# A three-block kernel on one core: query tokens, rotary product, gate product and column sums are computed another way, and three tables of work order are new

## What is computed

```
proj = h @ w_in                                  # h: 528 x 1024
p_rwkv, p_diff, p_gate = split(proj)
# RWKV branch: the gate
g = sigmoid(gd) @ g2                             # gd: 528 x 160, g2: 160 x 1024
y = (y + bonus) * g
# differential attention, 8 heads, each with two score maps
q, k = partial_rope(q), partial_rope(k)          # the first 16 of 64 rows of each half head turn
x1, x2 = x[..., :8], x[..., 8:16]
rot = [x1 * cos - x2 * sin, x2 * cos + x1 * sin]
o = concatenate([meta_out, outs])                # queries 0..15, then 4 blocks of 128 queries
merged = gates0 * (o_rwkv @ W) + gates1 * (o_diff @ W')
h_res = h_res + merged @ w_out
h = rms_norm(h_res)                              # needs the sum over 1024 rows of h_res**2
h_res = h_res + square(relu(h @ w1)) @ w2
out = rms_norm(h_res)[:, 16:]                    # the 16 meta tokens are dropped
```

## Time and profile before

| | |
|---|---|
| median of 3 runs | 3085.76 us (3073.72 to 3088.74) |
| profiled execution, its own time | 3070.59 us |
| its span | 3068.7 us |
| mean granted TensorE clock | 0.952 |

### The profile page before, as it was taken

How to read it: one execution, slowest core, us unless ns; L and a number is a source line. 1 busy time by engine, 2 the same in 40 slices (tenths; PEclk the granted TensorE clock), 3 DMA queues, 4 the chain that set the end, 5 groups by cost and what they waited for, 6 DMA issues and landing times.

```text
span 3068.7 us, 53994 instructions
## 1 busy us (share of the span) xinstructions
PE 2826.4 (92%) x22582; PEld 2275.8 (74%) x22582; DVE 1601.6 (52%) x2907; ACT 1215.1 (40%) x2134; POOL 849.2 (28%) x849
## 2 busy tenths in 40 slices
PE   7899999989998999999989988998897999899997
PEld 7788888878876877887667777776775888566565
DVE  4545644555432544343244446456666899844553
ACT  2423433342331233233242434353325777534341
POOL 5222222212224200000143535353100027454233
PEclk9989998999899999999998999999999999899999
DMA  4111111111114332333121212221433888421122
GB/s 140 36 33 42 34 40 36 39 29 40 39 51 172 117 110 89 96 95 91 51 66 52 80 51 77 63 76 55 158 100 123 327 318 335 167 76 56 42 59 69
DMA packets 104003, 286.24 MB, mean 93 GB/s; under 512 B 11696, under 2 KB 11824, under 8 KB 102480
## 3 DMA queue, kind: packets, MB, share of 16 engines
q1 hardware_dynamic: 83408, 209.11, 22.2%
q0 software_dynamic: 15024, 62.14, 5.5%
q10 hardware_dynamic: 5328, 11.54, 1.0%
HBM read 262.81 MB, written 19.92 MB: 92 GB/s over the span
## 4 chain that ended last, share of the span: by engine, by line
PE 70%; DVE 17%; ACT 9%; issue 2%; DMA 2%; ACTq 0%; DVEq 0%; SPq 0%; POOLq 0%
PE psum L497 68%; DVE arena L429 9%; ACT arena L414 4%; ACT arena L422 3%; DVE arena L438 3%; PE psum L501 2%; ACT L409 1%; DVE ring L429 1%; DMA ring<-in_w 1%; DVE arena L433 1%; DVE arena L441 1%; DVE arena L453 0%; DVE arena L450 0%; DMA arena<-in_x 0%; DVE arena L457 0%
## 5 line engine op out<-in xcount | busy, mean ns | idle before, releaser
L497 PE MATMUL psum<-arena,ring 128*128 128x512 f32 (+3 forms) x6280 | 1453.9, 365 | 16.9 <-DVE arena L429 6.0
L497 PEld LDWEIGHTS psum<-arena,ring 128*128 128x128 f32 (+2 forms) x6280 | 1047.3, 193 | 210.9 <-issue 36.8
L497 PE MATMUL psum<-arena 32*32 32x32 f32 (+18 forms) x12332 | 798.8, 244 | 138.2 <-DVE arena L429 46.1
L497 PE MATMUL psum<-arena,arena 128*128 128x512 f32 (+2 forms) x3004 | 844.3, 386 | 37.0 <-DVE arena L429 15.1
L497 PEld LDWEIGHTS psum<-arena 32*32 32x32 f32 (+10 forms) x12332 | 581.4, 136 | 322.1 <-issue 113.4
L497 PEld LDWEIGHTS psum<-arena,arena 128*128 128x128 f32 x3004 | 541.4, 189 | 171.4 <-issue 25.2
L441 POOL CAST ring<-ring 128x512 fp32r<-128x512 f32 x348 | 234.6, 674 | 1357.1 <-DMA ring<-in_w 1213.5
L422 ACT ACTIVATE arena<-psum 128x512 f32<-128x512 f32 (+12 forms) x682 | 295.3, 450 | 752.0 <-PE psum L497 598.4
L429 DVE TENSOR_TENSOR arena<-arena 128x256 f32<-128x256 f32 (+8 forms) x681 | 361.8, 544 | 229.7 <-ACT arena L414 115.9
L429 POOL TENSOR_TENSOR ring<-ring,ring 128x512 fp32r<-128x512 f32 x348 | 465.8, 1338 | 28.0
L414 ACT ACTIVATE arena<-arena 128x512 f32<-128x512 f32 (+10 forms) x532 | 305.2, 583 | 343.0 <-DVE arena L429 160.9
(11 more groups left out here) (52 smaller groups left out, 843.6 us busy)
## 6 DMA issues: line engine op xcount, KB each, us to landing
ring<-in_w SPq DMA_DIRECT2D x372, 256.0 KB, 2.7
ring<-in_w SPq DMA_DIRECT2D x133, 512.0 KB, 3.5
arena<-in_w SPq DMA_DIRECT2D x61, 512.0 KB, 5.5
bg<-arena ACTq DMA_DIRECT2D x24, 256.0 KB, 2.2
yd<-arena ACTq DMA_DIRECT2D x7, 512.0 KB, 7.2
arena<-bg POOLq DMA_DIRECT2D x1, 3072.0 KB, 16.8
arena<-in_x SPq DMA_DIRECT2D x1, 2112.0 KB, 8.1
od<-arena POOLq DMA_DIRECT2D x8, 256.0 KB, 2.3
```

The source lines that it names most:

```text
L497: self.last_ins = self.eng.matmul(out, l, r, start=start, stop=stop, skip_group_check=skip)
```

## The change

Seven parts:

1. Queries of the 16 meta tokens are no longer computed in the attention: q is projected for 512 tokens in one bank (24 matmuls of 512 columns in place of 48 of 264), the 16-query tile goes, and the head's last column sum is over 512 tokens.
2. Rotary: the product with `rot` goes; four small DMAs, issued by ACT after its copy, move 8 rows each to their partner's place in `d.rot` (the signs are in `sin` now). `d.rot` shares the tile `d.P[3]`.
3. The gate's last 32 rows: weights and activations are laid out three times on 96 rows (high, high, low on high, low, high) and multiplied once in fp32r. The third low-rank tile is computed with 96 rows in place of 32, and DVE makes the parts once (7 instructions) before the heads begin.
4. The MLP's first column sum: POOL adds tiles 0 to 6, PE sums two operands in place of 8.
5. The sums at the MLP's end: POOL adds tiles 0 to 6 of squares and of values; PE does 4 matmuls in place of 16. POOL's clearing of the mixers' accumulators waits for these sums as well.
6. The mean after the branches of block 2: POOL adds tiles 0 to 6; PE does 2 matmuls in place of 8.
7. `WORK`, `BESIDE`, `LEAD` (9 to 8) and `ORDER` have other entries. `BESIDE` adds up to 216 in place of 240 steps; `ORDER` has as many d, l and g as before.

```
@@ pack_params
-    rows("g2b", g2[128:])
+    rows("g2b", np.tile(g2[128:], (3, 1)))
...
@@ tables
-LEAD = 9
+LEAD = 8
...
@@ pe_rwkv
+            P.wait_ge(*at("g2_parts"))
...
-            P.mm(o, p["g2b"][0:32, 128 * hp:128 * hp + 128], m.lora[2][0:32, J], False, True)
+            P.mm(o, m.g2_r[0:96, 128 * hp:128 * hp + 128], m.lora_r[0:96, J], False, True)
@@ dve_rwkv
+    V.wait_ge(*at("lora_act", 2))
+    V.cp(m.part_r[32:64, 0:T], m.lora[2][32:64])
+    V.apart().cp(m.part_r[64:96], p["g2b"][64:96])
+    V.tt(m.lora_r[32:64], m.lora[2][32:64], m.part_r[32:64, 0:T], SUB)
+    V.apart().cp(m.lora_r[0:32], m.lora[2][0:32])
+    V.apart().cp(m.lora_r[64:96], m.lora[2][64:96])
+    V.apart().cp(m.g2_r[0:64], p["g2b"][0:64])
+    V.apart().tt(m.g2_r[64:96], p["g2b"][64:96], m.part_r[64:96], SUB, "g2_parts")
@@ pe_diff
-TK = [(0, 16)] + [(16 + 128 * j, 128) for j in range(4)]
+TK = [(META + 128 * j, 128) for j in range(4)]
...
+                if n == 2:
+                    pe_terms(K, m, b, wh(k), wl(k), kx)
+                else:
+                    P.mm3([ps[:, 512 * b:512 * b + tokens]], wh(k), wl(k), m.hx_r[kx], m.lx_r[kx], kx == 0, kx == 7)
...
-            P.colsum(("df_rot", nme, hd), ("df_sin", nme, hd), c["rot"], [d.q if nme == "q" else d.k], T, [("df_qk", nme, hd)])
...
-        for i in range(5):
+        for i in range(4):
@@ act_diff
+            if hd or i:
+                A.wait_ge(*(at("df_roped", "q", hd) if i else at("df_roped", "k", hd - 1)))
+            n = x.shape[1]
+            for r, (to, of) in enumerate(zip(swapped(d.rot), (1, 0, 3, 2))):
+                A.ready().dma_start(to[:, 0:n], swapped(x)[of]).then_inc(*K.book.up("df_rot", ("df_rot", nme, hd, r), by=16))
@@ dve_diff
-            V.apart().wait_ge(*at("df_rot", nme, hd))
-            V.apart().tt(h2(d.t2), out_of(K, 2, T, "df_sin", nme, hd), h2(c["sin"]), MUL, "df_sin", nme, hd)
-            V.tt(x, d.t1, d.t2, ADD, "df_roped", nme, hd)
+            V.apart().wait_ge(*at("df_rot", nme, hd, 3))
+            V.apart().tt(d.t2[:, 0:n], d.rot[:, 0:n], c["sin"][:, o:T], MUL)
+            V.tt(x, d.t1[:, 0:n], d.t2[:, 0:n], ADD, "df_roped", nme, hd)
@@ pool_gates
+    for k in range(1, 7):
+        if k == 1:
+            G.wait_ge(*at("sq", "mlp", 0))
+        G.wait_ge(*at("sq", "mlp", k))
+        G.tt(m.odh[:, 0:T], m.odh[:, 0:T], m.odh[:, k * T:k * T + T], ADD, "mg_sq", k)
+    for k in range(1, 7):
...
+        G.wait_ge(*at("xsq", k))
+        G.tt(m.sqx[:, 0:T], m.sqx[:, 0:T], m.sqx[:, S], ADD)
+        G.tt(m.acc_out, m.out[:, 0:T] if k == 1 else m.acc_out, m.out[:, S], ADD, "mg_x", k)
@@ pe_branches
-            pe_add(K, b, m.h[:, (k - 1) * T2:k * T2], k - 1, "b_h", k - 1)
-    pe_add(K, b, m.h[:, 7 * T2:8 * T2], 7, "b_h", 7)
+    K.P.colsum(("mean", "ln1"), ("centred", "ln1", 7), K.c["ones"], [m.h_acc, m.h[:, 7 * T2:8 * T2]], T2, [("b_hacc", 6), ("b_h", 7)])
```

More of the change, by code:

```diff
@@ L52, in constants @@
     cos, sin = np.ones((128, T1)), np.zeros((128, T1))
-    rot = np.zeros((128, 128))
     for h in (0, 64):
@@ L56, in constants @@
             cos[h + j] = cos[h + 8 + j] = np.cos(ang[:, j])
[L57 to L60, removed]
+            sin[h + 8 + j] = np.sin(ang[:, j])
+            sin[h + j] = -sin[h + 8 + j]
+    c["cos"], c["sin"] = cos, sin
     m = np.ones((128, T1)); m[:, ::CH] = 0
@@ L965, in pe_rwkv @@
     P, at, ps, p, c, T = K.P, K.book.at, K.ps, K.p, K.c, T1
-    for i, rows in enumerate((128, 128, 32)):
+    for i, rows in enumerate((128, 128, 96)):
         b = P.bank(2, "lora_sh", i)
@@ L1638, in scores @@
             for q, k, meta, rest, most in half:
-                P.mm(meta, c["ident16"][0:16, 0:16], c["negm16"][0:16, 0:16], False, True)
+                P.mm(rest[:, 0:W - 144], q, k[:, 16:W - 128])
         else:
-            if nb == 2:
-                for q, k, meta, rest, most in half:
-                    P.mm(meta, q, k[:, 0:16])
-                for q, k, meta, rest, most in half:
-                    P.mm(rest[:, 0:W - 144], q, k[:, 16:W - 128])
-            else:
-                for q, k, meta, rest, most in half:
-                    P.mm(most, q, k[:, 0:W - 128])
@@ L1649, in scores @@
-            for q, k, meta, rest, most in half:
-                P.mm(rest[:, W - 144:W - 16], q, k[:, W - 128:W], True, False)
-            for q, k, meta, rest, most in half:
-                P.mm(rest[:, W - 144:W - 16], c["ident16"][:], c["negm16"][:], False, True)
+            for q, k, meta, rest, most in half:
+                P.mm(most, q, k[:, 0:W - 128])
+        for q, k, meta, rest, most in half:
+            P.mm(rest[:, W - 144:W - 16], q, k[:, W - 128:W], True, False)
+        for q, k, meta, rest, most in half:
+            P.mm(rest[:, W - 144:W - 16], c["ident16"][:], c["negm16"][:], False, True)
@@ L1665, in values @@
+        m0, n0 = weights_at(b, i)
+        P.tr(ps[0:META, m0:m0 + 128], aw[:, 0:META])
+        for j in range(i + 1):
+            P.tr(ps[:, n0 + 128 * j:n0 + 128 * j + 128], aw[:, TK[j][0]:TK[j][0] + 128])
         P.did("df_tr", hd, i)
@@ L1752, in act_diff @@
         b = bank_of(K, "df_V", hd)
-        A.apart().copy(d.V[0:16, 0:128], ps[0:16, 512 * b:512 * b + 128])
+        A.apart().copy(d.V[0:META, 0:128], ps[0:META, 512 * b:512 * b + 128])
         A.apart().copy(d.V[:, 128:640], ps[:, 512 * b + 512:512 * b + 1024], "df_V", hd)
@@ L1795, in dve_diff @@
         V.cp(c[n + "16"][:], c[n], *(("masks",) if n == "negm" else ()))
+    V.apart().ms(d.rot, 0.0)
+    V.apart().ms(d.am, 0.0)
+    V.apart().ms(d.V[:, 0:128], 0.0, "df_zero")
     V.apart().tt(m.lt, p["lq1"], p["lk1"], MUL)
@@ L2006, in pe_mlp @@
             if i == 2:
-                pe_sum8(K, "mlp", m.odh, T)
+                P.colsum(("sum", "mlp"), ("root", "mlp"), K.c["ones"], [m.odh[:, 0:T], m.odh[:, 7 * T:8 * T]], T, [("mg_sq", 6), ("sq", "mlp", 7)])
         for k in range(8):
@@ L3108, in pool_mixers @@
     G.wait_ge(*at("end", "dve", "block1"))
+    G.wait_ge(*at("mean", "ln0"))
     for r in range(6):
@@ L3218, in pool_branches @@
         G.tt(m.y_r[k][:], m.x[:, k * T:k * T + T], m.Oh_r[k][:], SUB, "b_ylow", k)
+    for k in range(1, 7):
+        if k == 1:
+            G.wait_ge(*at("b_h", 0))
+        G.wait_ge(*at("b_h", k))
+        G.tt(m.h_acc, m.h[:, 0:T] if k == 1 else m.h_acc, m.h[:, k * T:k * T + T], ADD, "b_hacc", k)
 BLOCKS, PAIRS, EQ = 7, 4, ALU.is_equal
```

192 lines of the change are left out of this document (94 added, 98 removed).

## The result

| | before | changed |
|---|---|---|
| median of 4 runs each | 3085.24 us (3073.72 to 3088.74) | 2976.19 us (2971.91 to 2985.91) |
| ratio, 95% interval | 1 | 0.966 (0.962 to 0.969) |
| span of the profiled execution | 3068.7 us | 2970.1 us |
| mean granted TensorE clock | 0.952 | 0.956 |

The account below looks back on a forecast made before the run. PE, busy 92% of the span, was taken as the bound. Heads 22 us plus MLP and branches 20.6, tables 0, made 42.6 us off the median 3085.76: 3043 us, range 3015 to 3072.

Parts of the forecast that it names:

- No row prices this ... 0 as the value: New digits in the heads and new ORDER in the mixers: no reason for a sign, so 0 us counted.
- the 44 that I held possible: Heads and mixers: a third of PE's idle time, 44 us either way, as the ends of the tables' range.
- the orders fit better: Rival, 10%: a third of 133 us of idle time in heads and mixers goes, 2999 us.
- Heads' edits: Heads: 29.0 us off PE's list, 27 coming through, less 5 of rotary waits: 22 us gained.
- the gate: Heads: 16 gate matmuls go from 0.42 us to the split price 0.124, saving 4.8 us.
- Rotary path: Heads: product's 13.4 us leave PE; the DMA path of 3.5 us costs 0.3 us of wait each, 5 us.
- its rival (3150 us): Rival "Slower", 5%: in the heads DVE's wait for the rotary DMAs holds PE, 112 us less 47.6.
- Sums: MLP and branches: 24 fp32 products leave PE, 20.6 us; MLP shorter by 15.5, branches by 5.
- Clock: Heads: 14% at half clock, so removed work might count 33 us in place of 29; 29 kept.
- the line I drew: The forecast is wrong if the low clock's share moves by a third.
- My argument on idle time and the clock: Heads: the low clock does not take idle time; at 468 to 475 PE was busy throughout and stood at 0.50.

Follow-up runs that it names:

- the old places: Changed kernel with the heads' tables of before, less the dropped query tile's 24 steps in BESIDE, ORDER new: 3016.42 us, ratio 0.975 to before.
- the old heads tables: Changed kernel with WORK, BESIDE and LEAD of before, 240 steps handed out for 216: 3090.92 us, ratio 1.005 to before.
- the run with 16 meta rows: Changed kernel with the first product of the weighted values on 16 rows again in place of 128: 2975.87 us, ratio 0.965 to before.

## Why the prediction was wrong

- **Tables.** The step that failed is "No row prices this ... 0 as the value". The heads' digits are worth 21 us against the same steps at the old places (28 by the rate), and `ORDER` 15 to 20 (21 us of idle time, 84.2 to 63.4 on the old code and 82.7 to 61.2 on the new, less some 3 us of work). Together they are some 40 us, near the 44 that I held possible, and all on one side. I gave "the orders fit better" 10%; it had the right mechanism and nearly the right size, but at 2999 us it still lies 23 us above what was measured. The second half of the error is that I took tables and edits as separate: with the old digits the edits made the heads 16 us longer clock-free (839 to 855; by the rate 22) and 51 us longer as measured. New digits were not an extra but a condition, since `BESIDE` must add up to the steps that exist; the sign could have been read from that.
- **Heads' edits.** Forecast 22 us at given places, measured 16 to 18. That the total is near is partly luck, since its parts erred against each other. Work fell by 38 and not 29 us: the gate gave 9.5 in place of 4.8, since I priced its products by a row of another kind, and the padded meta product 2.6 that I had not listed; the 2 us left are no more than equal programs differ by. Idle time rose by 21 where I had 7 (29.0 - 27, and 5 of waits).
- **Rotary path.** 13.4 us off PE, 5 us of waits: net 8.4 forecast, 3 to 9 measured with the new digits and 11 at the old places (by the rate 8 and 5). The path is longer than I had it (4.6 us in place of 3.5), and its rival (3150 us) did not come: PE's idle time in the heads is 61.1 us against 62.6 before.
- **Sums.** Confirmed. From 981 to 1518 before, 925 to 1446 after: 537 to 521 us, 16 where I said 15.5; POOL's sums are late by 1.3 us in two waits of PE. The branches took 4 us off, forecast 5.
- **Clock.** The heads spent 119 us at the low clock before and 85 after, worth 16 us (12 by the rate), which I kept out of the sum. This is the second step that failed, the largest after the tables. Equal heads differ by up to 55 us in it (85 to 140), so one profile can't say how much of it is the change's. It is not a third (34 of 119 is 29%), but near the line I drew.
- **My argument on idle time and the clock** leaned on one window, and is refuted as a rule. In the heads of before, PE was busy less than 90% of the 7 us ahead of 14 of the 17 falls of the clock, and 9 of 13 in the changed kernel; of all stretches of 7 us in the same stage only 30 and 25 in a hundred are so. (The 7 us are my choice, to see what PE did before a fall.) So falls go with idle time, which my argument had denied, but 3 of the 17 and 2 of the 13 came after 7 us without any. One of each kind from the changed kernel, 7 us and what followed:

```profile
263.00:270.00 7.00, 3.73 (x41) 2.62 (x42) 6.02 (x9) 0.00 (x0) 6.62 (x7) 1.00 0.27 75
270.00:276.00 6.00, 6.00 (x50) 4.60 (x49) 1.25 (x6) 0.00 (x0) 0.63 (x1) 0.53 0.01 3
738.00:745.00 7.00, 7.00 (x120) 6.24 (x120) 2.87 (x6) 4.74 (x8) 0.00 (x0) 0.98 0.14 40
745.00:748.00 3.00, 3.00 (x16) 1.86 (x18) 2.70 (x6) 2.77 (x5) 0.00 (x0) 0.50 0.00 0
```

In the first, PE was busy 3.73 of 7 us at 2.4 GHz and then stood at 1.2 GHz; in the second it had been busy throughout and fell as well. The Trainium skill, "TensorE: Matmul & The Clock Gate", section "HAM oscillation — how this bites in real kernels", says that idle gaps bring the clock down; most falls here agree, and the fully busy ones do not. What it means for the sum is in the table: with the old heads tables 60 us more of idle time came with 116 us more at the low clock, so in this pair of kernels an idle microsecond cost 1.7 to 1.9. That the idle time caused the low clock there is likely by the falls, and not shown by itself.

Summed by what was measured, clock-free: edits in the heads 18, digits 21, `ORDER` 15 to 20 and sums 19 to 20 make 73 to 79 us; the heads' clock adds 16, which leaves 4 to 10 of the spans' 98.6, about what equal programs differ by. By the rate the heads alone are 16 + 28 + 12 = 56, of their 56.5.

## What to carry to other kernels

Where a change removes steps from a list that is handed out by a table, the new table is part of the edit: price the edit at fixed places, then ask what the table can win back, with PE's idle time as its size and gain as the likelier sign. Compare profiles by idle time plus work at the full clock, since the low-clock time differs by tens of us between executions of one program, and test such a measure on equal programs first. Price a product by the pitch in its own place in the trace, not by a like one elsewhere. A product taken off the bounding engine is worth its pitch only while something else fills the waits that it had covered: three edits here, each undone by itself, changed the total by less than could be measured.

## What the hardware showed

- A DMA issue of 8 rows within the chip's own memory took ACT 631 ns, against 326 ns for the 256 KB ones of the earlier trace rows; four are 3.2 us of ACT's queue the first time and 2.6 the second (at 69.62 in the changed kernel).
- The pitch of an fp32 product depends on its neighbours. Records of 264 columns come every 0.22 us where 128-row products follow one another, and every 0.31 to 0.33 in the gate, where products of 128 and 32 rows alternate. Around the 16-row product of the run with 16 meta rows they come every 0.20 to 0.21 us, and between 128-row ones of the same 128 columns every 0.11. That it is the change of row count was not tried by itself. The fp32r products of 96 rows in the changed kernel:

```profile
L495 PE MATMUL psum<-arena,arena 96*128 96x264 f32 x16 | 7.7, 481 | 0.0
```

- At the low clock the split matmuls of 264 columns start 228 ns apart against 128 at the full one: less than twice.
